# A two-block transformer kernel on one core: transfers, row sums and squares in another order

## The reference

```
mod = silu(c) @ w_ada + b_ada                      # 9 vectors of 1024
n = rmsnorm(h) * (1 + scale) + shift;  h += 0.5 * gate * swiglu(n)        # FFN 1, width 2816
n = modulate(rmsnorm(h));              h += gate * mixer(n)               # "pool" mixer, 8 heads + pooling
n = modulate(rmsnorm(h));              h += 0.5 * gate * swiglu(n)        # FFN 2
x = rmsnorm(h)
for layer in (window, causal):                     # 16 heads each
    q, k, v, z = rmsnorm(h) @ w_in;  o = attention(rope(q), rope(k), v) * silu(z);  h += o @ w_out
out = rmsnorm(h)
```

## Time and profile before

| | us |
|---|---|
| median of 3 runs | 784.79 |
| the runs | 785.63, 778.40, 784.79 |
| the profiled execution | 790.26 |
| its span, first to last instruction | 788.5 |
| its mean granted TensorE clock | 0.975 |

### The profile page before, as it was taken

How to read it: one execution, slowest core, us unless ns; L and a number is a source line. 1 busy time by engine, 2 the same in 40 slices (tenths; PEclk the granted TensorE clock), 3 DMA queues, 4 the chain that set the end, 5 groups by cost and what they waited for, 6 DMA issues and landing times.

```text
span 788.5 us, 14860 instructions
## 1 busy us (share of the span) xinstructions
PE 730.4 (93%) x6128; PEld 685.1 (87%) x6128; DVE 528.7 (67%) x733; ACT 366.7 (47%) x564; POOL 129.1 (16%) x80
## 2 busy tenths in 40 slices
PE   5699999999998999877999999999999988999984
PEld 4488999999997988667999999999888788988884
DVE  3588977888857446438659558546789966678831
ACT  4253334434345355425343434446666665565632
POOL 0052212322232816104005000001300000000000
PEclk9799999999999999978999999999999999999997
DMA  9996798877649990419657664754443334343301
GB/s 309 349 309 220 247 347 301 287 252 233 210 157 296 351 315 1 150 41 313 218 173 254 220 206 139 233 166 153 143 126 108 107 108 160 107 161 110 106 1 53
DMA packets 132454, 152.62 MB, mean 194 GB/s; under 512 B 2616, under 2 KB 126268, under 8 KB 132284
## 3 DMA queue, kind: packets, MB, share of 16 engines
q1 hardware_dynamic: 132324, 152.01, 59.2%
q10 hardware_dynamic: 88, 0.02, 0.0%
HBM read 150.97 MB, written 1.05 MB: 193 GB/s over the span
## 4 chain that ended last, share of the span: by engine, by line
PE 71%; DVE 12%; ACT 9%; DMA 3%; issue 3%; POOL 1%; SPq 0%; DVEq 0%; ACTq 0%; POOLq 0%
PE sc L1346 10%; PE sc L1348 10%; PE sc L1347 10%; PE acc L1346 9%; PE acc L1348 9%; PE acc L1347 9%; DVE wlo L913 4%; ACT whi L603 3%; PE stat L1357 2%; DMA ada<-in_w_ada_dram 2%; ACT probT L736 1%; DMA raw<-in_w_gate_dram 1%; DVE vp L1095 1%; PE acc L1604 1%; PE acc L1605 1%
## 5 line engine op out<-in xcount | busy, mean ns | idle before, releaser
L913 DVE TENSOR_TENSOR wlo<-raw,whi 128x2048 fp32r<-128x2048 f32 x105 | 258.6, 2466 | 117.5 <-ACT whi L603 117.0
L603 ACT ACTIVATE whi<-raw 128x2048 fp32r<-128x2048 f32 x105 | 200.2, 1907 | 82.7 <-PE sc L1348 61.4
L1346 PE MATMUL sc<-nhi,whi 128*128 128x256 f32 x704 | 199.7, 284 | 7.8 <-DVE nlo L950 4.0
L1347 PE MATMUL sc<-nlo,whi 128*128 128x256 f32 x704 | 199.1, 283 | 0.0
L1348 PE MATMUL sc<-nhi,wlo 128*128 128x256 f32 x704 | 199.0, 283 | 0.0
L1346 PEld LDWEIGHTS sc<-nhi,whi 128*128 128x128 f32 x704 | 133.8, 190 | 9.1 <-issue 6.1
L1347 PEld LDWEIGHTS sc<-nlo,whi 128*128 128x128 f32 x704 | 135.4, 192 | 0.0
L1348 PEld LDWEIGHTS sc<-nhi,wlo 128*128 128x128 f32 x704 | 135.0, 192 | 0.0
L1346 PE MATMUL acc<-nhi,whi 128*128 128x256 f32 x376 | 109.8, 292 | 5.7 <-DVE nlo L950 2.8
L520 POOL TENSOR_TENSOR ada<-ada,cpad 128x2048 f32<-128x2048 f32 x15 | 71.5, 4777 | 234.0 <-DMA ada<-in_w_ada_dram 201.5
L1348 PE MATMUL acc<-nhi,wlo 128*128 128x256 f32 x376 | 104.5, 278 | 0.0
(11 more groups left out here) (219 smaller groups left out, 1149.1 us busy)
## 6 DMA issues: line engine op xcount, KB each, us to landing
ada<-in_w_ada_dram SPq DMA_DIRECT2D x28, 1024.0 KB, 6.2
raw<-in_w_gate_dram SPq DMA_DIRECT2D x22, 1024.0 KB, 5.9
raw<-in_w_up_dram SPq DMA_DIRECT2D x22, 1024.0 KB, 5.6
raw<-in_w_down_dram SPq DMA_DIRECT2D x22, 1024.0 KB, 4.9
raw<-in_w_out_dram SPq DMA_DIRECT2D x12, 1024.0 KB, 5.0
raw<-in_w_in_b_dram SPq DMA_DIRECT2D x10, 1024.0 KB, 5.1
raw<-in_w_in_a_dram SPq DMA_DIRECT2D x9, 1024.0 KB, 5.3
raw<-in_w_in_dram SPq DMA_DIRECT2D x8, 1024.0 KB, 9.0
```

Of the source, the lines that this page charges most:

```text
L603: nc.scalar.activation(whi[:, u % NS], raw[:, u % NS], ACT.Copy).then_inc(hi_done, 1)
L913: nc.vector.tensor_tensor(wlo[:, u % NS], raw[:, u % NS], whi[:, u % NS].bitcast(F32), ALU.subtract).then_inc(lo_done, 1)
L1346: mm(to, stat_hi, mov_hi, start=first, stop=False, skip_group_check=True)
L1347: mm(to, stat_hi, mov_lo, start=False, stop=False, skip_group_check=True)
```

## The change

- **Transfers.** In SyncE's queue the transfers of slice 31, of the final gain and of the sinks move from the end of the pool mixer's list to behind the second FFN's first gate and up units.
- **Pool mixer's output stage.** ROW30 stands ahead of OUT3. VectorE copies row 31 after the list instead of in it, and takes `mod_out(30)` and the third coefficient behind the reciprocal of the norm instead of ahead of it.
- **End of FFN 1.** Three column sums (12 to 14) stay between the down products, four (15 to 18) and the sum 19 go behind the sums of squares; row 19 goes ahead of the sums of squares of chunks 4 and 5; VectorE copies row 20 after the norm.
- **Window mixer's output stage.** The unit that OUT2 split is split behind OUT3's residual.
- **The end.** The root table is loaded behind the first output bank, each bank is squared as it is done, VectorE multiplies each bank by the final gain into `xo`, and after the reciprocal VectorE scales three parts of `xo` and ScalarE the fourth.

```
-                     "TPV1", "OUTB", "MOD26", "ROW28", "OUT1", "ROW29", "OUT2", "MOD28", "OUT3", "ROW30", "ROW31",
+                     "TPV1", "OUTB", "MOD26", "ROW28", "OUT1", "ROW29", "OUT2", "MOD28", "ROW30", "OUT3", "ROW31",
...
                     load_unit(base, gate[:, :, 0:UC])
                     load_unit(base + 1, up[:, :, 0:UC])
+                    load_ada(31)
+                    sp.dma_start(fgain[:, :], final_g_2.rearrange("(a n) -> a n", a=1).to_broadcast([P, D])
+                                 ).then_inc(late_in, 16)
+                    sp.dma_start(sinks[:, :], sinks_a_2.to_broadcast([P, 16])).then_inc(late_in, 16)
                     load_ada(32)
...
-                                 3 * FB + 10: (30,), 3 * FB + 11: (31,)}
+                                 3 * FB + 10: (30,)}
...
-                if first:
-                    sp.dma_start(fgain[:, :], final_g_2.rearrange("(a n) -> a n", a=1).to_broadcast([P, D])
-                                 ).then_inc(late_in, 16)
-                    sp.dma_start(sinks[:, :], sinks_a_2.to_broadcast([P, 16])).then_inc(late_in, 16)
...
-                sp.wait_ge(res_out, j + 1)
+                if j < 3:
+                    sp.wait_ge(res_out, j + 1)
+                else:
+                    sp.wait_ge(last_out, 1)
...
+            def final_squares(j):
+                for b in range(2):
+                    ins = nc.scalar.activation((sq, tn)[j // 2][:, 2 * (j % 2) + b],
+                                               out_acc["last"][j][:, b * S:(b + 1) * S], ACT.Square,
+                                               accum_out=fss[:, b, j:j + 1])
+                ins.then_inc(fss_done, 1)
...
-                        if j < 3 or name == "causal":
+                        if name == "causal" or j < 2 or j == 2 and name == "pool":
                             high(st["u"] + NS)
+                        elif name == "window" and j == 3:
+                            high(st["u"] - 1 + NS)
+                        if name == "causal":
+                            if j == 0:
+                                load_sqrt(7)
+                            final_squares(j)
...
-            load_sqrt(7)
-            for j in range(4):
-                act.wait_ge(fin_mm, j + 1)
...
             act.wait_ge(fsum_done, 1)
             nc.scalar.activation(fst[:, 1], fst[:, 0], ACT.Sqrt, bias=tiny[:, 1:2], scale=1.0 / D).then_inc(fstd_done, 1)
+            act.wait_ge(finv_done, 1)
+            act.wait_ge(gained, 4)
+            for b in range(2):
+                to = xo[:, b, 3 * UC:4 * UC]
+                ins = nc.scalar.activation(to, to, ACT.Copy, scale=fst[:, 2, b:b + 1])
+            ins.then_inc(last_out, 1)
...
             def normalise(k):
                 inverse_deviation(k)
...
+                elif k == 2:
+                    mod_out(30, mod2_ps)
+                    dve.wait_ge(mod_done, 32)
+                    link(coefficient(2))
...
+            def final_gain(j):
+                dve.wait_ge(fss_done, j + 1)
+                for b in range(2):
+                    cols = slice(j * UC, (j + 1) * UC)
+                    ins = nc.vector.tensor_tensor(xo[:, b, cols], out_acc["last"][j][:, b * S:(b + 1) * S], fgain[:, cols],
+                                                  ALU.mult)
+                ins.then_inc(gained, 1)
...
-                        if st["i"] < 3 or name == "causal":
+                        if name == "causal" or st["i"] < 2 or st["i"] == 2 and name == "pool":
                             low(st["u"] + NS)
+                        elif name == "window" and st["i"] == 3:
+                            low(st["u"] - 1 + NS)
+                        if name == "causal" and st["i"] < 3:
+                            final_gain(st["i"])
...
                 if f == 0:
                     copy_late_row(19)
-                    copy_late_row(20)
...
             normalise(1)
+            copy_late_row(20)
             copy_late_row(21)
...
             mixer("pool")
-            dve.wait_ge(mod_done, 32)
-            link(coefficient(2))
+            copy_late_row(31)
             normalise(2)
...
             nc.vector.tensor_reduce(fst[:, 0], fss[:, :, :], AX_X, ALU.add).then_inc(fsum_done, 1)
+            final_gain(3)
             dve.wait_ge(fstd_done, 1)
-            link(nc.vector.reciprocal(fst[:, 2], fst[:, 1]))
-            for j in range(4):
...
+            nc.vector.reciprocal(fst[:, 2], fst[:, 1]).then_inc(finv_done, 1)
+            dve.wait_ge(finv_done, 1)
+            dve.wait_ge(gained, 4)
+            for j in range(3):
+                for b in range(2):
+                    to = xo[:, b, j * UC:(j + 1) * UC]
+                    ins = nc.vector.tensor_scalar(to, to, fst[:, 2, b:b + 1], None, ALU.mult)
                 ins.then_inc(res_out, 1)
...
-                    if f == 0 and m < 7:
-                        mod_sum(12 + m, mod2_ps[:, 2 * m:2 * m + 2])
+                    if f == 0 and m in (1, 3, 5):
+                        n = m // 2
+                        mod_sum(12 + n, mod2_ps[:, 2 * n:2 * n + 2])
                 if f == 0:
                     pe.wait_ge(mod_done, 12)
                     sum_squares(1, None, True)
+                    late_rows(19)
                     sum_squares(1, 4, False)
                     sum_squares(1, 5, False)
-                    late_rows(19)
                     sums_after(1)
+                    for n in range(3, 7):
+                        mod_sum(12 + n, mod2_ps[:, 2 * n:2 * n + 2])
+                    mod_sum(19, mod2_ps[:, 14:16])
                     pe.wait_ge(res_done, DC * 1 + 6)
                     late_rows(20)
-                    mod_sum(19, mod2_ps[:, 14:16])
                     late_rows(21)
```

More of the change, by code:

```diff
@@ L364, in build @@
         res_out = sem("res_out")
+        gained = sem("gained")
+        finv_done = sem("finv_done")
+        last_out = sem("last_out")
         out_sent = sem("out_sent")
@@ L884, in _ @@
             mixer("causal")
-            load_sqrt(7)
-            for j in range(4):
-                act.wait_ge(fin_mm, j + 1)
-                for b in range(2):
-                    ins = nc.scalar.activation((sq, tn)[j // 2][:, 2 * (j % 2) + b],
-                                               out_acc["last"][j][:, b * S:(b + 1) * S], ACT.Square,
-                                               accum_out=fss[:, b, j:j + 1])
-                ins.then_inc(fss_done, 1)
             act.wait_ge(fsum_done, 1)
             nc.scalar.activation(fst[:, 1], fst[:, 0], ACT.Sqrt, bias=tiny[:, 1:2], scale=1.0 / D).then_inc(fstd_done, 1)
+            act.wait_ge(finv_done, 1)
[4 more added lines that the diff above has]
+            ins.then_inc(last_out, 1)
         @block.vector
@@ L1186, in mixer @@
                             input_low(5, 2 * st["i"] + 1)
-                        if st["i"] < 3 or name == "causal":
+                        if name == "causal" or st["i"] < 2 or st["i"] == 2 and name == "pool":
                             low(st["u"] + NS)
+                        elif name == "window" and st["i"] == 3:
+                            low(st["u"] - 1 + NS)
+                        if name == "causal" and st["i"] < 3:
+                            final_gain(st["i"])
+                    elif kind == "ROW" and st["i"] < 31:
+                        copy_late_row(st["i"])
                     elif kind == "ROW":
-                        copy_late_row(st["i"])
-                    elif kind == "MOD":
-                        mod_out(st["i"], mod2_ps if st["i"] == 30 else mod3_ps)
+                        pass
+                    elif kind == "MOD" and st["i"] < 30:
+                        mod_out(st["i"], mod3_ps)
                     before = st
@@ L1329, in _ @@
             nc.vector.tensor_reduce(fst[:, 0], fss[:, :, :], AX_X, ALU.add).then_inc(fsum_done, 1)
+            final_gain(3)
             dve.wait_ge(fstd_done, 1)
-            link(nc.vector.reciprocal(fst[:, 2], fst[:, 1]))
-            for j in range(4):
+            nc.vector.reciprocal(fst[:, 2], fst[:, 1]).then_inc(finv_done, 1)
+            dve.wait_ge(finv_done, 1)
+            dve.wait_ge(gained, 4)
+            for j in range(3):
                 for b in range(2):
-                    ins = nc.vector.scalar_tensor_tensor(
-                        out=xo[:, b, j * UC:(j + 1) * UC], in0=out_acc["last"][j][:, b * S:(b + 1) * S],
-                        scalar=fst[:, 2, b:b + 1], in1=fgain[:, j * UC:(j + 1) * UC], op0=ALU.mult, op1=ALU.mult)
+                    to = xo[:, b, j * UC:(j + 1) * UC]
+                    ins = nc.vector.tensor_scalar(to, to, fst[:, 2, b:b + 1], None, ALU.mult)
                 ins.then_inc(res_out, 1)
```

## The result

| | before | after |
|---|---|---|
| median of 5 runs, us | 782.86 | 762.79 |
| the runs, us | 778.40 to 785.63 | 762.33 to 767.02 |
| the profiled execution, us | 790.26 | 767.02 |
| its span, us | 788.5 | 765.2 |
| its mean granted clock | 0.975 | 0.982 |

The ratio is 0.9746 (95% interval 0.9701 to 0.979), so 16 to 23 us are won. The forecast of 766.0 and its range hold. The traced execution of the kernel before is a slow one (1.5% above its fastest run); experiment 8 traces the same kernel again at a span of 781.2 us and has the same lengths, within 0.1 us, in all stages of the change.

The account below looks back on a forecast made before the run. TensorE, busy 93% of 788.5 us, was the bound; only its idle time, low-clock time and tail could be won. Terms 9.2 + 2.9 + 4.2 + 4.0 = 20.3 us, carried to the median, gave 766.0 us, range 759 to 774.

Parts of the forecast that it names:

- pool output stage: Pool mixer's output stage: earlier weight transfers shorten the row-copy wait, the clock stays up, the reciprocal starts earlier; 9.2 us.
- the forecast's 0.35: Pool mixer's output stage: reciprocal starts at once, with two small VectorE operations behind it; 0.35 us won.
- end of FFN 1: End of the first FFN: moved sums and row copies let the norm's reciprocal start earlier; 2.9 us.
- causal start: Start of the causal mixer: residual ahead of the split removes a 2.5 us wait and the low clock behind it; 4.2 us.
- tail: After the last product: table, squares and gains of three banks move under TensorE's output products; 4.0 us.
- Rival A: Whole kernel: low clock absent from the runs shown, or stays, so only waits are won; 769.1 us, chance 0.15.
- Rival B: Pool stage: late transfers of weights or slices hold it, losing 2.9 us again; 769 us, chance 0.08.
- D: Pool output stage: something else keeps the gate weight until 325, only 11 us won; 774 us, chance 0.04.
- C: Before the second FFN: the clock's fall goes too, 2.5 us more won; 763.5 us, chance 0.12.
- E: Pool output stage and stages behind: clock stays at 1.2 GHz, making the kernel slower; 785 to 790 us, chance 0.03.
- so the reciprocal starts at 235.75 instead of 238.64: End of the first FFN: without row 20's copy first, the norm's reciprocal starts earlier; 2.9 us won.
- a third of a difference: From profiled execution to median: a third of the difference between 764.5 and 769.1, for low clock, giving 766.0 us.

Follow-up runs that it names:

- experiment 8: The kernel before, unedited, traced a second time: 782.98 us, span 781.2 us.
- experiment 4: Changed kernel with the old end restored (root table, squares and gain behind all four banks): ratio 0.9829 to the kernel before.
- experiment 1: Changed kernel with slice 31, final gain and sinks back ahead of the second FFN's first weights in SyncE's queue: ratio 0.9861 to the kernel before.
- experiment 7: Changed kernel with ROW30 behind OUT3, and mod_out(30) and the third coefficient ahead of the reciprocal again: ratio 0.9752 to the kernel before.
- experiment 6: Changed kernel plus 26 unused products on TensorE filling the wait before the second FFN: ratio 0.9765 to the kernel before.
- experiment 5: Changed kernel with VectorE's copy of row 19 waiting for only 12 column sums instead of 18: ratio 0.977 to the kernel before.
- experiments 3: Changed kernel with the window mixer's last split ahead of OUT3's residual again: ratio 0.9808 to the kernel before.
- experiment 10: Changed kernel with row 19's copy freed, 26 filler products, and slices 32 and 33 transferred behind the second FFN's second weights: ratio 0.9774 to the kernel before.

## Why the prediction was right, point by point

The stages of the change, with the forecast, the difference between the two first traces, and what undoing the part alone gave back. The pool output stage is counted to the first normalised chunk, since the forecast's 0.35 already has the two operations behind the reciprocal in it:

| term | forecast | from the table | part undone |
|---|---|---|---|
| pool output stage | 9.2 | 8.8 | 8.1 (transfers) + 0.1 (order) |
| end of FFN 1 | 2.9 | 1.4 | 1.3 |
| causal start | 4.2 | 4.4 | 4.6 |
| tail | 4.0 | 3.8 | 3.8 |
| sum | 20.3 | 18.4 | 17.9 |

(Causal start and tail share the last three rows of the stages, 8.17 us in all; the tail's 3.8 is from experiment 4.)

- **Pool output stage: right, and for the reason given.** The residual, squares, high half, low half and copy came in the order of the forecast with 1.1 us of wait left (1.3), the clock stayed up, and experiment 1 undoes it with the transfers alone. The 0.35 us for the order of rows and reciprocal did not come (0.07 in experiment 7). Rival A is out: the mean granted clock was 0.962 to 0.975 in every run of the kernel before in the rounds of the experiments, so the runs have the low clock as the traced one has it, and 0.978 to 0.982 in the five of the changed kernel. Rival B is out: no wait of TensorE for a weight or a slice appeared between 230 and 360. D is out: the gate weight is issued at 297.66, which is my 304.0 less the 6.4 us by which this stage now begins earlier (316.88 against 323.29 for its first residual). C is out: the fall before the second FFN stayed, with a wait of 3.7 us, and experiment 6 shows that its removal would have given 0.9 to 1.0 us and not 2.5. E is out; the output stage stays at full clock in the changed kernel.
- **End of FFN 1: the direction right, the size half.** The step that failed is "so the reciprocal starts at 235.75 instead of 238.64". I followed the two row copies on VectorE only as far as row 20's, which the change moved away. Row 19's stayed, and it waits for 18 column sums, which the same edit moved behind the sums of squares: a wait on a count became late because what it counts had been moved. Experiment 5 measures this at 1.1 us. The other 0.4 us are the deviation: I had it at 235.2, 7.67 us behind the bias addition, and it starts at 8.06. TensorE's new 0.77 us wait for GpSimd's partial sum stands in that chain but is not what the forecast missed: experiment 5, at the wide spacing of the trace that I forecast from, has 8.07 without it. At least 0.2 us of it is my reading of the statistics: I took 0.95 us from the start of the last sums of squares to the deviation, where the trace of before has 1.17 (236.10 to 237.27). What the rest is stays open. Of the 2.8 us wait before the pool mixer 1.3 is left where the clock stays up, and its going was worth nothing by itself: the pool mixer lasts 84.60 against 84.65.
- **Causal start and tail: right.** The displaced split cost nothing. In the tail the six scalings took 1.67 us, 0.28 each, where I took 0.35 from bounds of 0.30 and 0.48: below my lower bound. The two squares took 0.84 and not 0.7.
- **From the profiled execution to the median: the number served, the reason was wrong.** I put the 5.5 us between the two down to the low clock, and took off a third of a difference built on it. Experiment 8 has the same mean clock as the first trace and lies 7.3 us under it. What differs is the spacing of products at full clock in one FFN. The clocks of the untraced runs (0.962 to 0.975) point the same way: they are not higher than the traced one's 0.975. The traced run of the change too lay over its median (767.02 against 762.79). The lengths of the stages carry over to the median without this term: 782.86 - 18.4 = 764.5, or 762.6 with my own 20.3, where 762.79 was measured. That my 766.0 came so near is partly luck: the sum was 1.9 us too large, and the 1.5 us that I took off the gain for a cause that was not there worked against that.

## What to carry to other kernels

When instructions move, list every wait on a count that they feed, on all engines, and ask for each waiting instruction what is queued behind it; a threshold written for the old order may then hold back work that needs nothing of what it waits for. When an operation moves across the mark to which a stage is measured, measure to a mark behind both. A gap filled so that the clock stays up pays only as far as the next engine can follow, here VectorE's 0.79 us a chunk. And before a trace's excess over the median is explained, compare the length of stages that the change doesn't touch: here 5 us of a difference of 23 lay in one.

## What the runs showed of the hardware

- **Product spacing has two values at full granted clock.** In the FFNs, products of 256 columns follow each other every 0.1133 us (a window of 20 us holds 178 or 179) or every 0.1178 (172 or 173), with TensorE busy throughout and the granted clock at 1.00 in both. It holds for long stretches and differs between executions of one kernel (experiment 8) and between stages of one (FFN 1 and FFN 2 of the changed kernel). It makes 6.8 us in one FFN, about as much as the medians' runs scatter; that it is the source of their scatter I infer, since the untraced runs leave only their time and mean clock. What sets it, the runs don't tell.
- **The place where the clock falls moves from execution to execution.** Beside a stretch near the start and one behind the last product, it is low in the changed kernel from 232.7 and from 341.9; in experiment 7 from 71.2, 235.1 and 344.3; in experiments 3, 4 and 6 there is no fall at the end of FFN 1 at all, though all of these have the same instructions on every engine up to there. The two traces of the kernel before fall in the same places. In the output stage of the pool mixer it fell in all three executions that have row 19's copy freed (at 319.5 and 315.4, behind waits of 0.6 to 0.9 us, and at 330.9, behind the 1.1 us for the row copy) and in no other that has the new transfers; why an earlier start by 1.1 us should do that stays open, and with three executions against six it may be chance. That the place is not tied to one wait agrees with the Trainium skill (TensorE: Matmul & The Clock Gate, "What's actually happening"), by which the monitor of activity runs freely.
- **A split on VectorE beside GpSimd** took up to 5.27 us instead of 2.29 in experiment 6 (3.36 + 5.27); in experiment 10, where the two splits start 1.2 us earlier behind the reciprocal, they took 10.17 together and ended at the same distance from it.
